# Differential attention heads: transposing the weights by DMA in halfword planes instead of on TensorE

## What is computed

```python
s1 = einsum('bqhd,bshd->bhqs', q1, k1) * scale + bias
s2 = einsum('bqhd,bshd->bhqs', q2, k2) * scale + bias
p = softmax(s1, axis=-1) - lam * softmax(s2, axis=-1)
o = einsum('bhqs,bshd->bqhd', p, v)
yb = rms_norm_2(o, b_subln_g, SUBLN_EPS) * (1.0 - lambda_init)
```

## Time and profile before

| | |
|---|---|
| median of 3 runs | 3058.57 us (3057.92 to 3058.85) |
| the profiled execution, its own time | 3058.66 us |
| span of the profile, first to last instruction | 3056.9 us |
| granted TensorE clock, mean | 0.999 of full |
| TensorE busy (matmul) | 3043.0 us |
| VectorE busy | 1869.1 us |
| ScalarE busy | 1469.8 us |
| GpSimd busy | 134.2 us |
| DMA, mean | 177 GB/s |

### The profile page before, as it was taken

The page is one execution under the profiler, slowest core; times in us unless marked ns, Lnnn a source line. Parts: engine busy times, 40 slices in busy tenths (PEclk is TensorE's granted clock), DMA queues, the critical chain, the costliest instruction groups (busy, mean ns, idle before and its releaser), DMA issues.

```text
span 3056.9 us, 48305 instructions
## 1 busy us (share of the span) xinstructions
PE 3043.0 (100%) x20906; PEld 2827.8 (93%) x20906; DVE 1869.1 (61%) x2263; ACT 1469.8 (48%) x1699; POOL 134.2 (4%) x132
## 2 busy tenths in 40 slices
PE   9999999999999999999999999999999999999999
PEld 9989999999999999989888888889998889999987
DVE  7775555445445557776565565556787666767663
ACT  5544433333333357755443443345565654555553
POOL 0001000000000011110000000002000001101000
PEclk9999999999999999999999999999999999999999
DMA  6334555555554554455555555554444545555554
GB/s 236 108 111 166 174 173 178 179 177 171 176 179 168 182 195 176 159 193 179 194 191 188 185 179 198 187 192 179 179 140 153 178 175 184 179 193 186 174 191 152
DMA packets 94516, 539.57 MB, mean 177 GB/s; under 512 B 25568, under 2 KB 26080, under 8 KB 31584
## 3 DMA queue, kind: packets, MB, share of 16 engines
q1 hardware_dynamic: 77264, 532.14, 50.0%
q10 hardware_dynamic: 17040, 4.34, 0.8%
HBM read 530.15 MB, written 2.10 MB: 174 GB/s over the span
## 4 chain that ended last, share of the span: by engine, by line
PE 97%; DVE 1%; ACT 1%; DMA 1%; issue 0%; SPq 0%; ACTq 0%; DVEq 0%
PE PB L1158 28%; PE PB L1159 15%; PE PB L1183 14%; PE PB L1182 14%; PE PB L1184 13%; PE PB L1177 2%; PE PB L1178 2%; PE PB L1179 2%; PE PB L1169 1%; PE PB L1168 1%; PE PB L1167 1%; PE PB L1240 1%; DMA raw<-in_mla_in 1%; PE PB L1308 1%; DVE WLt L1796 0%; PE PB L1309 0%
## 5 line engine op out<-in xcount | busy, mean ns | idle before, releaser
L1796 DVE TENSOR_TENSOR WLt<-raw,WHt 128x2048 fp32r<-128x2048 f32 (+2 forms) x506 | 1139.3, 2259 | 760.7 <-ACT WHt L1415 760.2
L1415 ACT ACTIVATE WHt<-raw 128x2048 fp32r<-128x2048 f32 (+2 forms) x506 | 955.0, 1890 | 1117.3 <-PE PB L1159 582.0
L1158 PE MATMUL PB<-Xt,WHt 128*128 128x512 f32 x2880 | 1027.6, 395 | 0.0
L1159 PE MATMUL PB<-Xt,WLt 128*128 128x256 f32 x2880 | 808.5, 281 | 0.0
L1158 PEld LDWEIGHTS PB<-Xt,WHt 128*128 128x128 f32 x2880 | 540.8, 188 | 109.8
L1182 PE MATMUL PB<-Xt,WHt 128*128 128x272 f32 (+1 forms) x2192 | 635.0, 290 | 2.8 <-DVE WLt L1796 1.9
L1183 PE MATMUL PB<-Xt,WHt 128*128 128x272 f32 (+1 forms) x2192 | 630.2, 287 | 0.0
L1184 PE MATMUL PB<-Xt,WLt 128*128 128x272 f32 (+1 forms) x2192 | 626.9, 286 | 0.0
L1159 PEld LDWEIGHTS PB<-Xt,WLt 128*128 128x128 f32 x2880 | 543.5, 189 | 0.1
L1182 PEld LDWEIGHTS PB<-Xt,WHt 128*128 128x128 f32 x2192 | 412.8, 188 | 12.6 <-DVE WLt L1796 4.9
L1183 PEld LDWEIGHTS PB<-Xt,WHt 128*128 128x128 f32 x2192 | 413.5, 189 | 1.1 <-issue 0.2
(11 more groups left out here) (268 smaller groups left out, 2858.1 us busy)
## 6 DMA issues: line engine op xcount, KB each, us to landing
raw<-in_gu SPq DMA_DIRECT2D x176, 1024.0 KB, 4.8
raw<-in_dn SPq DMA_DIRECT2D x88, 1024.0 KB, 4.8
raw<-in_odd_in SPq DMA_DIRECT2D x64, 1024.0 KB, 4.8
raw<-in_even_in SPq DMA_DIRECT2D x52, 1024.0 KB, 4.9
raw<-in_lru_in SPq DMA_DIRECT2D x24, 1024.0 KB, 4.9
raw<-in_mla_o SPq DMA_DIRECT2D x16, 1024.0 KB, 4.8
raw<-in_lru_o SPq DMA_DIRECT2D x16, 1024.0 KB, 5.0
raw<-in_even_o SPq DMA_DIRECT2D x16, 1024.0 KB, 4.9
```

What stands on the lines that cost most here:

```text
L1158: t.matmul(o, wh, both, start=first, stop=False)
L1159: m = t.matmul(o[:, 0, :], wl, ah, start=False, stop=last)
L1415: a.activation(hi, r, ACT.Copy).then_inc(s_hi, 1)
L1796: v.tensor_tensor(lo, r, hi.bitcast(f32), sub).then_inc(s_lo, 1)
```

## The change

Every differential head is transposed as the odd layer's are, with ScalarE in GpSimd's place for the planes. `t_` is gone and three steps stand for it:

- `x_(j)`, gaps 1 and 3: ScalarE splits `E1` into two planes of halfwords in `sqt` (`diff_planes`).
- `c_(j)`, gaps 2 and 4: ScalarE issues the transposing DMA from `sqt` to `acct` (`diff_cross`).
- `w_(j)`: ScalarE weaves the high halfwords, VectorE the low ones, into `TT2` or `TT3` (`diff_weave`). For the first head it stands in gap 2 between the two softmaxes of the second head, after `normed`; for the second head in gap 4, after the first head's product.

`weigh_rows` waits for both weaves instead of the PSUM copy. `p.mid` is as it was. The diff without the dispatch of the new steps to their functions:

```diff
     def diff_pair(q):
-        def s_(j):
+        def s_(j, between=None):
             hd = ("e", 8 + 2 * q + j)
...
                 if m == 0:
                     p.step("normed", hd, (hd, 0), "E1", False, 0)
+                    if between:
+                        between()
             p.mark("pp", "pp", hd)
             p.step("differ", hd)
             now["BB"] = now["E2"] = ("pp", hd)
 
         bufs = ("TT2", "TT3")
 
-        def t_(j):
-            t_step(("e", 8 + 2 * q + j), bufs[j])
+        def x_(j):
+            hd = ("e", 8 + 2 * q + j)
+            p.mark("diff planes", "diff planes", hd)
+            p.step("diff_planes", hd)
+            now["E1"] = ("diff planes", hd)
+
+        def c_(j):
+            p.step("diff_cross", ("e", 8 + 2 * q + j))
+
+        def w_(j):
+            hd = ("e", 8 + 2 * q + j)
+            p.mark("diff woven", "diff woven", hd, 1)
+            p.mark("diff woven low", "diff woven", hd, 0)
+            p.step("diff_weave", hd, bufs[j], now[bufs[j]])
...
-        if q < 3:
-            return {0: lambda: s_(0), 2: lambda: (t_(0), s_(1)), 4: lambda: (t_(1), v_(0)),
-                    5: lambda: (v_(1), q_(), n1_()), 6: n2_}
-        p.mid = lambda: (v_(1), q_())
-        return {0: lambda: s_(0), 2: lambda: (t_(0), s_(1)), 4: lambda: (t_(1), v_(0)), 5: n1_, 6: n2_}
+        sides = {0: lambda: s_(0), 1: lambda: x_(0), 2: lambda: (c_(0), s_(1, lambda: w_(0))), 3: lambda: x_(1),
+                 4: lambda: (c_(1), v_(0), w_(1)), 5: lambda: (v_(1), q_(), n1_()), 6: n2_}
+        if q == 3:
+            p.mid = lambda: (v_(1), q_())
+            sides[5] = n1_
+        return sides
...
+        DIFF_PLANES, DIFF_CROSSED = sqt[:, 0:512], acct[:, 0:512]
...
             def weigh_rows(hd, V, vj, b, vready):
                 bank = own("pv", hd)
-                t.wait_ge(*when("out", "tr", hd))
+                for i in range(2):
+                    t.wait_ge(*when("diff woven", hd, i))
...
+            def diff_planes(hd):
+                a.wait_ge(*when("pp", hd))
+                if hd[1] > 8:
+                    a.wait_ge(s_diff_crossed, 16 * (hd[1] - 8))
+                a.activation(DIFF_PLANES.bitcast(u16).rearrange("p (a n) -> p a n", a=2), halfwords(E1),
+                             ACT.Copy).then_inc(sems["diff planes"], 1)
+
+            def diff_cross(hd):
+                a.wait_ge(*when("diff planes", hd))
+                if hd[1] > 8:
+                    for i in range(2):
+                        a.wait_ge(*when("diff woven", ("e", hd[1] - 1), i))
+                x = DIFF_CROSSED.bitcast(u16).rearrange("p (g n) -> p g n", n=128)
+                a.dma_start(x, DIFF_PLANES.bitcast(u16), transpose=True).then_inc(s_diff_crossed, 16)
...
+            def diff_weave(hd, b, free):
+                a.wait_ge(s_diff_crossed, 16 * (hd[1] - 7))
+                if free:
+                    a.wait_ge(*when(*free))
+                a.activation(half_words(buf[b], 1), plane(DIFF_CROSSED, 1), ACT.Copy).then_inc(sems["diff woven"], 1)
...
+            def diff_weave(hd, b, free):
+                v.wait_ge(s_diff_crossed, 16 * (hd[1] - 7))
+                if free:
+                    v.wait_ge(*when(*free))
+                low = DIFF_CROSSED.bitcast(u16)[:, 0:512].rearrange("p (q k n) -> p k q n", q=2, k=2)
+                v.tensor_copy(buf[b].bitcast(u16).rearrange("p (k q n a) -> p a k q n", k=2, q=2, a=2)[:, 0],
+                              low).then_inc(sems["diff woven low"], 1)
```

More of the change, by code:

```diff
@@ L1029, in build_program @@
             ctx.enter_context(nc.semaphore(f"s_{n}")) for n in ("par", "cst", "lams", "tabA", "tabB", "last_gain", "out"))
+        s_diff_crossed = ctx.enter_context(nc.semaphore("s_diff_crossed"))
         s_crossed = ctx.enter_context(nc.semaphore("s_crossed"))
@@ L1614, in turn_split, with plane, half_words @@
                 a.activation(TTH, PB[bk][:, :], ACT.Copy).then_inc(sems["trh"], 1)
+            def diff_planes(hd):
[11 more added lines that the diff above has]
+                a.dma_start(x, DIFF_PLANES.bitcast(u16), transpose=True).then_inc(s_diff_crossed, 16)
+            def plane(x, i):
+                return x.bitcast(u16)[:, 512 * i:512 * i + 512].rearrange("p (q k n) -> p k q n", q=2, k=2)
+            def half_words(x, i):
+                return x.bitcast(u16).rearrange("p (k q n a) -> p a k q n", k=2, q=2, a=2)[:, i]
+            def diff_weave(hd, b, free):
[3 more added lines that the diff above has]
+                a.activation(half_words(buf[b], 1), plane(DIFF_CROSSED, 1), ACT.Copy).then_inc(sems["diff woven"], 1)
             def crossed(hd):
@@ L1733, in _ @@
                     crossed(*x)
+                elif what == "diff_planes":
+                    diff_planes(*x)
+                elif what == "diff_cross":
+                    diff_cross(*x)
+                elif what == "diff_weave":
+                    diff_weave(*x)
                 elif what == "uq_out":
```

## The result

The changed kernel takes 3078.48 us, median of 4 runs (3075.28 to 3079.76), against 3058.24 us before: +20 us, a ratio of 1.0065 with a 95% interval of 1.0052 to 1.0077. The forecast was 3060.1 us and no change that can be told. The execution profiled took 3077.31 us, with a span of 3075.5.

The account below looks back on a forecast made before the run. TensorE was taken to bound the kernel, with 97% of the last chain. The pairs' changes, +0.9 - 0.87 - 0.87 + 2.35 = +1.5 us on 3058.57, gave 3060.1 us; range 3054.9 to 3063.5 us, own bounds 3059 to 3062.5.

Parts of the forecast that it names:

- Part 1: Gaps 2 and 4: 32 transposes leave TensorE, 0.87 us in each of four pairs, -3.5 us.
- full-duration rival: Each transpose frees its whole 272 ns of TensorE's queue, 8.7 us in all: 3050 us, chance 0.03.
- Part 2: Per head, ScalarE gets a plane split (1.2 us) and a weave, VectorE a weave; the DMA lands 2.7 us after issue.
- the f32 line: ScalarE's f32 instruction times, 0.63 us for 512 elements and 1.91 for 2048, giving the plane split at least 1.06 us.
- lands 2.7 us after that: Transposing DMA lands 2.7 us after its issue from ScalarE's queue, a time read from the odd layer's rows.
- Part 3: Gap 2: VectorE's weave between the two softmaxes adds 0.42 us to the chain, with no stall of TensorE.
- Nobody waits: Gap 2: first head's DMA lands at 2371.5, before its weave is due at about 2373.8.
- Part 4: Gap 4: V comes later; TensorE waits 1.8 us in the first pair, not in the second and third.
- Part 5: Last pair's second product, inside the unit behind gap 4: TensorE waits 3.2 us for the weave, starting 2.35 us later.
- Late landing: DMAs beside weight loads land late, deciding from 4.6 us: from about 3066, 3075 at 6.5; 0.13 with unseen stalls.
- the unseen stalls: A stall not foreseen in a queue behind the new waits; shares the chance of 0.13 with late landing.
- The bounds: Plane split at either end (-0.5, +0.8) and landing at 3.7 us (+1.0): 3059 to 3062.5 us.

Follow-up runs that it names:

- the version shown above: Changed kernel with the very last head on TensorE, first head's DMA at gap 1, second head's plane split and DMA behind the V copies: 3058.52 us.
- the idle-DMA pair: Kernel before plus eight transposing DMAs whose data nobody reads, issued beside weight loads (3060.51 us) or away from them (3058.33 us).
- the idle version: Kernel before plus eight transposing DMAs at gaps 2 and 4, beside weight loads, whose data nobody reads: 3060.51 us.
- second heads alone: Changed kernel with only the second head of each pair transposed by DMA, the first on TensorE as before: 3061.82 us.

## Why the prediction was wrong, point by point

- *Part 1, transposes off TensorE, -3.5 us.* Right. At gap 2 the scores now start 0.21 us behind the last weight matmul (2369.85 to 2370.06), and the pair without waits, in the version shown above, is 0.9 us shorter, forecast 0.87. The full-duration rival, 8.7 us, has no support.
- *Part 2, the added work.* The plane split takes 1.04 us (1037/1040/1042 ns), the f32 line's lower bound and not my 1.2; the weaves are as in the odd layer. **The step that failed is "lands 2.7 us after that".** I took the landing from the odd layer's row as if it were the DMA's own property. It was measured where the loads were elsewhere: in the odd layer a load was issued 5.7 us before the first transposing DMA of a pair and the next 1.4 us after it, here, in the second pair, 1.4 us before and 0.8 us after. Measured: 4.2 to 10.6 us. The odd layer even had one such neighbour: a transposing DMA at 2867.10, issued 0.9 us behind a load, took 5.6 us. The trace of before had all of it: low halves end at 2367.8 and 2370.0 in the second pair, and each end releases a load. I never laid those times beside the DMA's issue. The Trainium skill says in one line (Trainium Kernel Development and Optimization, "Key Constraints") that DMAs issued from the queues of SyncE, ScalarE and GpSimd run on the same 16 DMA engines and interleave; the idle-DMA pair, 7.6 against 3.1 us in the median, agrees that the two queues are not independent. The line has no price for it.
- *Part 3, 0.42 us for the weave between the softmaxes.* "Nobody waits" rested on the landing and fell with it: waits of 5.7 and 6.5 us there in the second pair. With short landings it holds, since the kernel with all else unchanged and the loads held has no wait in TensorE from this place. I also guarded the wrong resource: the PSUM bank of the scores ran out before the low half of a weight unit.
- *Part 4, V late in the first pair, 1.8 us.* A wait for V is there in the right pair, 1.15 us. V was done at 2331.40 in a pair that began 0.6 us sooner, so 1.3 us later than before and not the forecast 1.5; the shorter plane split gives that difference. It explains 0.2 of the 0.65 us by which the wait is shorter than forecast, and the rest stays open. The other wait for V, also 1.15 us, stands in the third pair, behind a landing of 7.3 us, where I had none. With the first heads' landings short it came in the second pair (0.9 us).
- *Part 5, 3.2 us of wait inside the last pair's unit.* The right place: 3.7 us. By accident: the DMA was issued earlier than I thought, right behind the table load (2498.38) and before the SiLU ran (2498.45), but took 4.2 us.
- *The rivals.* Late landing is what happened, and it had 0.13 with the unseen stalls. It put the deciding point at 4.6 us and 3075 us at landings of 6.5; measured were 5.8 us in the median and 3078.5. Its +17 us isn't the sum of its own terms, which is 1.5 + 3.8 + 8.4 and four times 1 to 1.5, so 18 to 20. "Once each in 16" overlooked the landing of 5.6 us. Its argument against, a median of 2.7 us, was the same error a second time: "issued beside the weight loads" was in the text as a condition, and I never looked whether it was met.
- *The bounds.* The terms named (-0.5, +0.8 and +1.0) give 3059.6 to 3061.9 us, not 3059 to 3062.5; it changes nothing.
- *Not in any case:* the low clock after a standstill, 5.1 of the 20 us.

## What to carry to other kernels

A landing time read from a trace belongs to the traffic around it. Before a DMA is put on a chain of waits, list the issues of all other queues some us before and after its new place, and price it by rows with the same neighbours. A step that waits for a DMA costs what stands behind it in the queue of its engine, so it goes where that engine has slack, and between two halves of a dependent chain only if the landing comes before its turn (with the DMA issued sooner, the weave between the softmaxes was no slower than the one at gap 3: 3058.5 and 3058.9 us); and to tell whether the DMA or the wait is at fault, issue the DMA with nobody waiting.

## What the runs showed of the hardware that I had not expected

- A transposing DMA of 256 KB beside 1 MB loads took 3.9 to 13.9 us in the idle version and 3.0 to 3.5 away from them; the load beside it took 10.7 us in the changed kernel, 6.7 in the same place before. The loads aren't the whole of it. Where they were held back, most landings were of 3.0 to 3.2 us, but five of 4.0 to 4.4; and of eight DMAs in the odd layer before, all with the same distances to the loads, seven took 2.7 or 2.8 us and one 6.5. What made these late stays open.
- At the end of the 10.7 us the DMA engines had little to do: over 2379.3 to 2381.3 their share of busy time was 0.06, at 25 GB/s. A share of 0.06 is one engine of 16. From 2378.83 to 2381.35 the trace has packets of 8 KB one behind the other, 0.31 us each, all of the load: it looks as if one engine still had its part of it to move when the fifteen others were done. The transposing DMA's last data packet had ended at 2378.96, but two small packets of it ended only at 2379.81 and 2380.13, between those of the load, and it landed at 2380.66. Why one engine fell behind stays open.
- TensorE's granted clock was at half for 3.4 us after each of the three standstills of 3.7 to 4.0 us. Their length alone doesn't decide: in other kernels of this case it fell to 0.50 as well after 2.25 us (loads held beside both heads), 2.35 us (very last head on TensorE, weave between the softmaxes) and 2.70 us (second heads alone), and stayed at 1.00 after 2.30 us (weave at gap 3) and 3.24 us (order kept, loads held).
- ScalarE's queue issued a DMA before operations ahead of it had run: at 2388.81, while the SiLU ahead of it started at 2388.89 and the high half at 2389.42.
